# Score levels of a decayed scan: two heads in one product, with the odd heads' tokens held in reverse order

## The chip, the cores and the metric

The kernel runs on one core of a Trainium2 chip. The metric is the device time of one execution in microseconds; lower is better. The engines of the core work side by side and meet at semaphores: TensorE (PE; its weight loads are PEld), VectorE (DVE), ScalarE (ACT), GpSimd (POOL) and SyncE (SP), which issues loads.

## The reference, cut to what matters

The whole program is two transformer-like blocks over 1024 tokens of width 1024. The second block holds an HGRN2 scan (8 heads of 128 key channels and 128 value channels), which the change rewrites:

```python
def hgrn2_chunkwise(q, fpre, v, lb):      # S_t = diag(f_t) S_{t-1} + (1 - f_t) v_t^T,  o_t = S_t^T q_t
    q = silu(q)
    f = lb + (1 - lb) * sigmoid(fpre)     # per channel
    k = 1 - f
    logf = log(f)
    # per chunk, b = cumsum(logf):
    #   A[t, s] = sum_d q[t, d] * exp(b[t, d] - b[s, d]) * k[s, d]      for s <= t
    #   o       = (q * exp(b)) @ S + A @ v
    #   S       = exp(b_last) * S + (k * exp(b_last - b))^T @ v
```

The difference b[t] - b[s] is taken per channel, so A isn't one plain product of q and k. The reference uses chunks of 64 tokens; the kernel uses tiles of 128.

## The kernel before

The program is a list of stages; each engine has its own instruction list, and the classes below write them through their methods pe, act and dve. Weights are streamed: SP loads a strip of 256 columns, GpSimd splits it into a high and a low part (a cast, L2671, and a subtraction, L2673, for each half of the strip), and TensorE makes every projection of three products (L217 and L401). A strip's first product on TensorE frees the buffer of the strip before, and GpSimd then starts to split the next one.

**Feeding stage (HgInputs).** It makes, transposed (channels on partitions, 512 tokens along the free axis, one job for each head and half of the tokens), q = silu (ScalarE, L1894), k = 1 - f (VectorE, L1943) and b = a running sum of log f that restarts at each tile of 128 (VectorE's scan, L1945). Each goes to the scratch tensor hT_s in HBM (L1863). The constants of the later stages (LATE) are loaded here, from ScalarE's queue (L1874).

**The scan (Hgrn).** Eight tiles of 128 tokens, all eight heads side by side in tiles of 128 x 1024. A is built from seven levels: at level l the tokens are cut into blocks of 2 x 2^l, and only pairs (query in the upper half of a block, key in the lower) are taken. With mid = b at the last token of the lower half, the two factors exp(mid - b) on the keys and exp(b - mid) on the queries are both at most one. VectorE subtracts (L2170 elo for keys, L2171 eup for queries), ScalarE takes Exp over the whole buffer E (L2051), VectorE multiplies with k and q (L2177 klo, L2178 kup) into KQ, TensorE multiplies KQ of every head by itself (L2116, a0 to a6: eight f32 products of 128 x 128 x 128, each in two records in the trace), and VectorE copies the wanted places from PSUM into A under a mask (`pick`, L2212; A is cleared once a tile, L2160). a7 is k by q unchanged, for the diagonal. E, KQ and the PSUM pair are double-buffered by the level's parity, so VectorE runs subtract(l), multiply(l-1), pick(l-2) in turn.

Then, once a tile: qe = q exp(b) (L2185), kdif (L2186), an Exp (L2072), kd (L2188), eight transposes of kd (L2122, kdT), their copy back to SBUF (L2075, kdr), the output products (L2131 and L2132, o), the state products (L2137, ds), the head norm (L2080 on ScalarE, small steps, L2199 `on`), the state update (L2204), the store of `on` to m_s (L2089), and the loads of q, k, b of two tiles ahead (L2040, three DMAs) and of v (L2043). The stores and loads all stand in ScalarE's list.

**What fills TensorE meanwhile (Units).** 208 units, each one tile of 128 tokens by 256 columns of the remaining projections (24 products, L217), are laid out by hand between the scan's products: marks(t) says how many units are made before each of a0..a7, the transposes, o and the next tile. From tile 1 on there is one unit between two levels, three between a7 and the transposes, one between these and o, five behind o. Each unit goes to one of two PSUM banks and ScalarE copies it out (L1985); TensorE can be at most two units ahead of that copy (`self.kept`). ScalarE's list has the copies at fixed places between its other work. The retention stage and the closing stage follow and take up the rest of the units.

## Time and profile before

| what | value |
|---|---|
| median of 3 runs | 3329.5 us (3325.21 to 3337.8) |
| the profiled execution's own time | 3327.03 us |
| its span | 3325.2 us |
| TensorE busy | 2998.3 us, 90% |
| VectorE busy | 1707.6 us, 51% |
| ScalarE busy | 689.0 us, 21% |
| GpSimd busy | 1099.5 us, 33% |
| granted TensorE clock, mean | 0.949 |

Busy time is the time in which an engine has an instruction under way, and it overlaps between engines; TensorE's products are pipelined, so it is not a measure of how hard the array works. In lists in order of time, the first number is the start in us from the span's start, the second the duration; what stands in square brackets is the engine's idle time before it and who ended it.

### The profile page before, as it was taken

How to read it: one execution, taken by the hardware profiler on the slowest of the kernel's cores; microseconds unless marked ns; L12 is line 12 of the kernel's file. 1: busy time of each engine (PE TensorE's matmuls, PEld its weight loads, DVE VectorE, ACT ScalarE, POOL GpSimd, SP SyncE). 2: the span in 40 equal slices, each digit the busy share in tenths (PEclk: the TensorE clock that was granted, in tenths of full speed). 3: DMA queues.
4: the chain of work that ended last, by engine and by line, in shares of the span. 5: the costliest groups of instructions: out<-in, count | busy, mean ns of one | idle time of the engine just before them, and what ended most of it. 6: DMA issues, size and time to landing. Idle time of an engine off the chain costs nothing.

```text
span 3325.2 us, 43694 instructions
## 1 busy us (share of the span) xinstructions
PE 2998.3 (90%) x18988; PEld 2703.1 (81%) x18988; DVE 1707.6 (51%) x2127; ACT 689.0 (21%) x1178; POOL 1099.5 (33%) x588
## 2 busy tenths in 40 slices
PE   6999777787899999999999897998999999989987
PEld 6888767776887887777777776778999999978887
DVE  3589356765331265444444448713166656455445
ACT  3010011221332231000000003311122222234331
POOL 7342131102553353232223323653223232311343
PEclk9998798988899999999999998999999999999998
DMA  5122221101431242111111114443333233345662
GB/s 194 56 91 87 77 70 51 39 29 35 160 114 51 83 145 90 38 39 50 38 38 51 51 38 146 152 158 114 96 115 109 83 106 105 127 147 182 228 241 89
DMA packets 148072, 325.71 MB, mean 98 GB/s; under 512 B 11148, under 2 KB 77608, under 8 KB 147752
## 3 DMA queue, kind: packets, MB, share of 16 engines
q10 hardware_dynamic: 105832, 169.80, 15.0%
q1 hardware_dynamic: 42048, 153.11, 14.7%
q8 instruction: 150, 2.46, 0.3%
q14 instruction: 42, 0.34, 0.0%
HBM read 245.26 MB, written 77.61 MB: 97 GB/s over the span
## 4 chain that ended last, share of the span: by engine, by line
PE 72%; DVE 13%; issue 5%; ACT 4%; POOL 2%; ACTq 2%; DMA 1%; DVEq 0%
PE pp L217 23%; PE pp L202 20%; PE pp L401 7%; PE pp L1609 6%; PE pp L2116 3%; POOL w_lo L2673 2%; PE pp L1151 1%; PE pp L1160 1%; PE pp L1162 1%; PE pp L1519 1%; DVE gdn_C L1343 1%; PE pp L1499 1%; DVE ffn_cb L557 1%; POOL w_hi L2671 1%; DVE gdn_U L1322 1%
## 5 line engine op out<-in xcount | busy, mean ns | idle before, releaser
L2671 POOL CAST w_hi<-w_raw 128x1024 fp32r<-128x1024 f32 x292 | 349.0, 1195 | 2176.7 <-PE pp L217 957.8
L217 PE MATMUL pp<-w_hi,act_hi 128*128 128x256 f32 (+1 forms) x2752 | 801.3, 291 | 51.6 <-ACT hg_st L1985 22.6
L217 PE MATMUL pp<-w_lo,act_hi 128*128 128x256 f32 (+1 forms) x2752 | 788.9, 287 | 0.0
L217 PE MATMUL pp<-w_hi,act_lo 128*128 128x256 f32 (+1 forms) x2752 | 788.8, 287 | 0.0
L2673 POOL TENSOR_TENSOR w_lo<-w_raw,w_hi 128x1024 fp32r<-128x1024 f32 x292 | 758.4, 2597 | 23.4
L217 PEld LDWEIGHTS pp<-w_hi,act_hi 128*128 128x128 f32 x2752 | 542.9, 197 | 59.3 <-issue 24.2
L217 PEld LDWEIGHTS pp<-w_lo,act_hi 128*128 128x128 f32 x2752 | 542.7, 197 | 0.0
L217 PEld LDWEIGHTS pp<-w_hi,act_lo 128*128 128x128 f32 x2752 | 541.9, 197 | 0.0
L202 PE MATMUL pp<-act_hi,w_hi 128*128 128x512 f32 x960 | 295.7, 389 | 1.6 <-POOL w_lo L2673 1.6
L202 PE MATMUL pp<-act_lo,w_hi 128*128 128x512 f32 x960 | 295.6, 389 | 0.0
L202 PE MATMUL pp<-act_hi,w_lo 128*128 128x512 f32 x960 | 295.5, 389 | 0.0
L401 PE MATMUL pp<-act_hi,w_hi 128*128 128x512 f32 x448 | 182.3, 407 | 33.8 <-ACT hgin_f L1859 16.8
L202 PEld LDWEIGHTS pp<-act_hi,w_hi 128*128 128x128 f32 x960 | 180.1, 188 | 39.2 <-issue 1.8
L202 PEld LDWEIGHTS pp<-act_lo,w_hi 128*128 128x128 f32 x960 | 180.2, 188 | 37.5
L202 PEld LDWEIGHTS pp<-act_hi,w_lo 128*128 128x128 f32 x960 | 180.2, 188 | 37.5
L2212 DVE COPY_PREDICATED hg_A<-up_masks,pp 128x1024 f32<-128x1024 int32 x64 | 87.1, 1362 | 190.4 <-issue 190.4
L401 PE MATMUL pp<-act_lo,w_hi 128*128 128x512 f32 x448 | 179.7, 401 | 0.0
L401 PE MATMUL pp<-act_hi,w_lo 128*128 128x512 f32 x448 | 179.6, 401 | 0.0
L1609 PE MATMUL pp<-w_hi,ffn_gh 128*128 128x512 f32 x352 | 119.8, 423 | 48.3 <-DVE ffn_y L1777 38.2
L862 DVE SCALAR_TENSOR_TENSOR mixin_conv<-pp,mixin_cw,mixin_conv 128x1023 f32<-128x1023 f32 (+14 forms) x120 | 152.0, 1267 | 3.7
L1777 DVE TENSOR_TENSOR ffn_y<-ffn_y,pp 128x1024 f32<-128x1024 f32 x72 | 87.1, 1218 | 106.9 <-PE pp L1609 106.9
L1985 ACT ACTIVATE hg_st<-pp 128x256 f32<-128x256 f32 x208 | 77.5, 378 | 265.4 <-PE pp L217 231.1
(382 smaller groups left out, 4469.9 us busy)
## 6 DMA issues: line engine op xcount, KB each, us to landing
w_raw<-in_weights SPq DMA_DIRECT2D x292, 512.0 KB, 3.7
z_s<-hg_st ACTq DMA_DIRECT2D x24, 1024.0 KB, 4.6
hg_qkb<-hT_s ACTq DMA_DIRECT2D x24, 512.0 KB, 6.2
qkvT_s<-mixin_o ACTq DMA_DIRECT2D x12, 512.0 KB, 2.8
gdn_qkv<-qkvT_s ACTq DMA_DIRECT2D x8, 768.0 KB, 5.1
front_x<-in_x ACTq DMA_DIRECT2D x8, 512.0 KB, 6.7
mix_x<-in_x ACTq DMA_DIRECT2D x8, 512.0 KB, 5.7
x_s<-mix_y ACTq DMA_DIRECT2D x8, 512.0 KB, 2.9
```

Of the source, the lines that this page charges most:

```text
L202: last = pe.matmul(dst[:, h * hn:(h + 1) * hn], w[slot][:, k * SC + mt * P:k * SC + mt * P + P], a[:, k, h * hn:(h + 1) * hn], start=(k == ...
L217: last = pe.matmul(dst, a[:, k, t * P:(t + 1) * P], w[slot][:, k * SC:k * SC + n], start=(k == 0 and a is high and w is w_hi), stop=(k == ...
L401: last = pe.matmul(dst, w[slot][:, k * SC + mt * P:k * SC + mt * P + P], a[:, k, h * 512:(h + 1) * 512], start=(k == 0 and w is w_hi and a ...
L557: ins = dve.scalar_tensor_tensor(dst[:, j:T], src[:, 0:T - j], w(k), dst[:, j:T], ALU.mult, ALU.add)
L862: ins = dve.scalar_tensor_tensor(dst[:, j:T], pp[3][:, 0:T - j], w, dst[:, j:T], ALU.mult, ALU.add)
L1609: last = pe.matmul(dst[:, h * 512:(h + 1) * 512], a[gset][:, kk, t * P:(t + 1) * P], w[slot][:, kk * D + h * 512:kk * D + h * 512 + 512], ...
L1777: self.sums.done(dve.tensor_tensor(y, y, new, ALU.add), "sum")
L1985: act.activation(self.st[i % 2][:, t, :], self.dst(k), ACT.Copy).then_inc(self.kept, 1)
L2116: last = pe.matmul(pp[l % 2][:, h * P:(h + 1) * P], lhs[:, h, :], rhs[:, h, :], start=True, stop=True)
L2212: self.dves.done(dve.copy_predicated(self.A[:, :, :], up_masks[:, l, :].rearrange("p (a n) -> p a n", a=1).broadcast_to((P, HH, P)), pp[l ...
L2671: pool.tensor_copy(hi, raw).then_inc(w_split, 1)
L2673: pool.tensor_tensor(lo, raw, hi.bitcast(F32), ALU.subtract).then_inc(w_ready, 1)
```

## The change

Only one half of the places of a level's product of a head with itself is used: queries are in upper halves, keys in lower ones. If another head's tokens are held in reverse order, its upper and lower halves change places, so one product can serve two heads: the stationary operand holds head j's keys in its lower places and the odd head's queries in the others, the moving operand the reverse. The change does this:

- The weights' columns of v, and the rows of hT_s, are ordered even heads first, odd heads behind (on the host, and by the store's address). Odd heads' q, k and b are written backwards within 512 tokens (`kept`), so a tile of an odd head is read from the mirrored place; the three loads of a tile become six of half the size.
- A level's operations on E and KQ are of the same sizes as before but take their operands from both halves with access patterns of one more dimension. At level 0 the keys' factor is one, so their subtraction is left out, the multiply is a copy, and Exp runs over half of E.
- a0 to a6 are four products; the picks copy 128 x 512 into a buffer `both` under masks that are symmetric. A is no longer cleared. a7 is unchanged.
- `join`: the diagonal of a7 into A by two multiplications with the identity, then two predicated copies out of `both`, upper places for even heads and lower ones, written backwards, for odd heads.
- qe is made in two operations, the odd heads' written backwards (so the queries of o are in true order).
- v of the odd heads is turned round by a product with a reversed identity (`turn_back`, jv) and copied back by ScalarE (vr); one of the five units behind o now stands between jv and o.
- The store of `on` becomes two stores which put the heads back into order.
- Small buffers move, one more constant is loaded in LATE, `both` is cleared once.

```diff
@@ LATE @@
-        LATE = [(up_masks, "c_up"), (ret_decay, "c_decay"), (ret_xi, "c_xi"), (ret_zeta, "c_zeta"), (ret_gc, "c_gc"),
+        LATE = [(up_masks, "c_up"), (turn_back, "c_back"), (ret_decay, "c_decay"), (ret_xi, "c_xi"), (ret_zeta, "c_zeta"), (ret_gc, "c_gc"),
...
+            def kept(self, x, j):
+                return backwards(x[:, :]) if j % 2 else x[:, :]
...
-                    self.qs.done(act.activation(self.q[j % 4][:, :], bank(2 * (j % 4)), ACT.Silu), "q")
+                    self.qs.done(act.activation(self.kept(self.q[j % 4], j), bank(2 * (j % 4)), ACT.Silu), "q")
...
-                    V.done(dve.tensor_scalar(self.k[s][:, :], f, -1.0, 1.0, ALU.mult, ALU.add), "k")
+                    V.done(dve.tensor_scalar(self.kept(self.k[s], j), f, -1.0, 1.0, ALU.mult, ALU.add), "k")
...
-                    V.done(dve.tensor_tensor_scan(self.b[s][:, :], self.keep[:, :], self.l[s][:, :], 0.0, ALU.mult, ALU.add), "b")
+                    V.done(dve.tensor_tensor_scan(self.kept(self.b[s], j), self.keep[:, :], self.l[s][:, :], 0.0, ALU.mult, ALU.add), "b")
@@ Hgrn.act @@
-                        act.dma_start(self.qkb[s][:, j, :, :], hT_s[j].rearrange("(h p) n -> p h n", p=P)[:, :, t * P:(t + 1) * P]).then_inc(self.loaded[s], 16)
+                        for odd in range(2):
+                            at = t if odd == 0 else t // 4 * 4 + 3 - t % 4
+                            heads = slice(odd * HH // 2, (odd + 1) * HH // 2)
+                            act.dma_start(self.qkb[s][:, j, heads, :], hT_s[j].rearrange("(h p) n -> p h n", p=P)[:, heads, at * P:(at + 1) * P]).then_inc(self.loaded[s], 16)
...
-                    after(act, V, f"eup{l}", t)
-                    A.done(act.activation(self.E[l % 2][:, :, :], self.E[l % 2][:, :, :], ACT.Exp), f"x{l}")
+                    after(act, V, f"er{l}", t)
+                    e = self.E[l % 2][:, :, :] if l else self.E[0][:, HH // 2:HH, :]
+                    A.done(act.activation(e, e, ACT.Exp), f"x{l}")
...
                     U.keep_to(act, m[9])
+                    after(act, PE, "jv", t)
+                    A.done(act.activation(self.v[t % 2][:, HH // 2:HH, :], bank(1).rearrange("p (h e) -> p h e", h=HH // 2), ACT.Copy), *(("xk", "kdr", "vr") if last else ("vr",)))
+                    U.keep_to(act, m[9] + 1)
                     after(act, PE, "o", t)
...
-                    act.dma_start(m_s[t * P:(t + 1) * P, :], self.on[:, :, :].rearrange("p h e -> p (h e)")).then_inc(self.stored, 16)
+                    for odd in range(2):
+                        act.dma_start(m_s[t * P:(t + 1) * P, :].rearrange("p (h two e) -> p h two e", two=2, e=P)[:, :, odd, :],
+                                      self.on[:, odd * HH // 2:(odd + 1) * HH // 2, :]).then_inc(self.stored, 16)
@@ Hgrn.pe @@
-                        for h in range(HH):
-                            last = pe.matmul(pp[l % 2][:, h * P:(h + 1) * P], lhs[:, h, :], rhs[:, h, :], start=True, stop=True)
+                        dst, keys = pp[l % 2], self.KQ[l % 2]
+                        if l < LEVELS:
+                            for j in range(HH // 2):
+                                last = pe.matmul(dst[:, j * P:(j + 1) * P], keys[:, j, :], keys[:, HH // 2 + j, :], start=True, stop=True)
+                        else:
+                            for h in range(HH):
+                                last = pe.matmul(dst[:, h * P:(h + 1) * P], self.qkb[s][:, 1, h, :], self.qkb[s][:, 0, h, :], start=True, stop=True)
...
+                    last = pe.matmul(bank(1), turn_back[:, :], self.v[s][:, HH // 2:HH, :].rearrange("p h e -> p (h e)"), start=True, stop=True)
+                    PE.done(last, *(("jv",) if t + 1 < NT else ("kdT", "jv")))
+                    U.make_to(pe, m[9] + 1)
+                    after(pe, A, "vr", t)
@@ Hgrn.dve @@
-                    V.done(dve.memset(self.A[:, :, :], 0.0), "zero")
...
-                            mid = bv[:, :, 0, sz - 1:sz].broadcast_to((P, nb, sz))
-                            V.done(tt(ev[:, :, 0, :], mid, bv[:, :, 0, :], ALU.subtract), f"elo{l}")
-                            V.done(tt(ev[:, :, 1, :], bv[:, :, 1, :], mid, ALU.subtract), f"eup{l}")
+                            mid = at_steps(b, sz - 1, rows(sz), [HALF_ + 1, 2], [0, sz])
+                            if l:
+                                V.done(tt(as_keys(e, sz), mid, of_keys(b, sz), ALU.subtract), f"el{l}")
+                            V.done(tt(as_queries(e, sz), of_queries(b, sz), mid, ALU.subtract), f"er{l}")
...
+                            if l:
+                                V.done(tt(as_keys(kq, sz), of_keys(k, sz), as_keys(e, sz), ALU.mult), f"klo{l}")
+                            else:
+                                V.done(dve.tensor_copy(as_keys(kq, sz), of_keys(k, sz)), "klo0")
+                            V.done(tt(as_queries(kq, sz), of_queries(q, sz), as_queries(e, sz), ALU.mult), f"kup{l}")
...
-                    self.pick(dve, t, LEVELS)
+                    self.join(dve, t)
...
+            def join(self, dve, t):
+                V, n = self.dves, HH // 2
+                raw = pp[LEVELS % 2][:, :].rearrange("p (h n) -> p h n", h=HH)
+                unit = ident[:, :].rearrange("p (a n) -> p a n", a=1).broadcast_to((P, n, P))
+                after(dve, self.pes, f"a{LEVELS}", t)
+                V.done(dve.tensor_tensor(self.A[:, 0:n, :], raw[:, 0:n, :], unit, ALU.mult), "dg0")
+                V.done(dve.tensor_tensor(backwards(self.A[:, n:HH, :]), raw[:, n:HH, :], unit, ALU.mult), "dg1")
+                after(dve, V, "dg1", t)
+                V.done(dve.memset(self.mark[:, :], 0.0), "ata")
+                V.done(dve.copy_predicated(self.A[:, 0:n, :], self.mask(LEVELS), self.both[:, :, :]), "cpa")
+                V.done(dve.copy_predicated(backwards(self.A[:, n:HH, :]), self.mask(LEVELS + 1), self.both[:, :, :]), "cpb")
```

## Rows read from the trace of the kernel before

**Rows 1.** The page, busy time and share of the span.
```profile
PE 2998.3 (90%) x18988; PEld 2703.1 (81%) x18988; DVE 1707.6 (51%) x2127; ACT 689.0 (21%) x1178; POOL 1099.5 (33%) x588
```
**Rows 2.** By stretches: us, PE, PEld, DVE, ACT, POOL busy, clock, DMA share, GB/s.
```profile
2487.53:2554.75 67.22, 66.79 (x569) 66.58 (x569) 42.39 (x64) 17.04 (x30) 18.23 (x8) 1.00 0.35 103
2554.75:2622.02 67.27, 66.78 (x568) 66.58 (x568) 42.37 (x63) 17.03 (x30) 18.23 (x8) 1.00 0.34 103
```
**Rows 3.** The chain that ended last, in time: start us, us, engine, line, records.
```profile
1101.09 3.46 PE pp L1499 x16
...
2507.53 1.78 PE pp L2116 x16
2509.31 2.88 PE pp L217 x24
```
**Rows 4.** Waits of TensorE, 2255 to 2890: total us, times, longest us.
```profile
PE pp L217 <- ACT hg_st L1985: 2.3, 6, 0.7
PE pp L2122 <- DVE hg_KQ L2188: 1.3, 1, 1.3
```
**Rows 5.** VectorE in one level, in time, and L2170 by itself (min/median/max ns).
```profile
2513.44 0.67 DVE L2178 TENSOR_TENSOR hg_KQ<-hg_qkb,hg_E 128x512 f32<-128x512 f32 x1
2514.05 1.34 DVE L2212 COPY_PREDICATED hg_A<-up_masks,pp 128x1024 f32<-128x1024 int32 x1
...
2515.30 0.67 DVE L2177 TENSOR_TENSOR hg_KQ<-hg_qkb,hg_E 128x512 f32<-128x512 f32 x1
...
L2170 DVE TENSOR_TENSOR hg_E<-hg_qkb x56: 628/678/2869, 2263.6 to 2845.7; 128x512 f32<-128x512 f32 x56
```
**Rows 6.** In time: VectorE beside GpSimd, within the levels of tile 2.
```profile
2502.95 2.70 POOL L2673 TENSOR_TENSOR w_lo<-w_raw,w_hi 128x1024 fp32r<-128x1024 f32 x1
2503.34 2.86 DVE L2177 TENSOR_TENSOR hg_KQ<-hg_qkb,hg_E 128x512 f32<-128x512 f32 x1
2506.12 0.68 DVE L2178 TENSOR_TENSOR hg_KQ<-hg_qkb,hg_E 128x512 f32<-128x512 f32 x1
```
**Rows 7.** In time: between a7 and the output products, tile 2.
```profile
2529.24 1.21 DVE L2185 TENSOR_TENSOR hg_KQ<-hg_qkb,hg_E 128x1024 f32<-128x1024 f32 x1
2530.37 1.21 DVE L2186 TENSOR_TENSOR hg_E<-hg_qkb 128x1024 f32<-128x1024 f32 x1
2532.57 2.40 POOL L2673 TENSOR_TENSOR w_lo<-w_raw,w_hi 128x1024 fp32r<-128x1024 f32 x1
2532.71 3.34 DVE L2188 TENSOR_TENSOR hg_KQ<-hg_qkb,hg_E 128x1024 f32<-128x1024 f32 x1 [1.13 <-ACT hg_E L2072]
2536.42 1.04 PE L2122 MATMUL pp<-ident,hg_KQ 128*128 128x128 f32 x8
2537.49 1.03 ACT L2075 ACTIVATE hg_E<-pp 128x1024 f32<-128x1024 f32 x1 [3.31 <-PE pp L2122]
```
**Rows 8.** Tile end: in time; L2040's three issues (min/median/max ns); then the chain.
```profile
2482.34 3.03 ACTq L2040 DMA_DIRECT2D hg_qkb<-hT_s  x3
2484.32 0.91 DVE L2160 MEMSET hg_A<- 128x1024 f32 x1 [0.38 <-DVE hg_S L2204]
2485.40 1.65 ACTq L2043 DMA_DIRECT2D hg_v<-z_s  x1
2489.07 0.69 DVE L2178 TENSOR_TENSOR hg_KQ<-hg_qkb,hg_E 128x512 f32<-128x512 f32 x1
...
L2040 ACTq DMA_DIRECT2D hg_qkb<-hT_s x3: 392/1062/1520, 2482.3 to 2483.9; - x3
...
2487.53 6.01 PE pp L217 x48
2493.55 1.78 PE pp L2116 x16
```
**Rows 9.** Feeding stage: L1943 by itself (min/median/max ns); one issue from the chain.
```profile
L1943 DVE TENSOR_SCALAR hgin_k<-hgin_f x16: 426/428/2505, 2080.3 to 2176.3; 128x512 f32<-128x512 f32 x16
...
2072.42 0.45 ACTq L1874
```

More of the change, by code:

```diff
@@ L147, in build @@
         late_end = top["at"]
+        spare = {"at": spare_at}
+        turn_back, both = place("turn_back", [P, P], F32, spare), place("both", [P, HH // 2, P], F32, spare)
         w_raw = place("w_raw", [P, STRIP])
@@ L187, in full, with backwards, at_steps @@
             return t[tuple(slice(None) for _ in t.shape)]
+        def backwards(x):
+            (step, n), off = x.ap[-1], x.offset
+            return bass.AP(x.tensor, off + step * (n - 1), [*[list(a) for a in x.ap[:-1]], [-step, n]])
+        def at_steps(x, first, *steps):
+            return bass.AP(x.tensor, x.offset + first, [list(x.ap[0]), *[list(a) for a in steps]])
         def weights_ready(pe, j):
@@ L2021, in __init__ @@
                 self.sm = b("sm", [P, 6, HH])
+                self.both = both
                 self.loaded = [sem(f"hg_loaded{s}") for s in range(2)]
@@ L2139, in pe @@
                     else:
-                        PE.done(last, "kdT", "o")
+                        PE.done(last, "o")
                     U.make_to(pe, m[10])
@@ L2723, in shape_constants @@
         low[:, l] = m
-        up[:, l] = m.T
-    up[:, LEVELS] = np.eye(P)
+        up[:, l] = m | m.T
+    up[:, LEVELS], up[:, LEVELS + 1] = np.triu(np.ones((P, P)), 1), np.tril(np.ones((P, P)), -1)
     h = np.arange(HH)
```

93 lines of the change are left out of this document (53 added, 40 removed).

## The prediction

> **What bounds the kernel now.** I read the page first: TensorE is busy for 90% of the span [rows 1]. Shares are an average over stages, so the second view is the table by stretches over the stage that is changed (2255 to 2892 us), cut at the same point of successive token tiles [rows 2]. A tile takes 67.22 us there, and TensorE is busy in 66.79 of them at granted clock 1.00, the upper of its two levels (2.4 GHz); VectorE in 42.39. So TensorE's instructions are the bound, and every one removed counts if nothing else comes due. The chain shows what they are [rows 3]: per level 1.78 us of score products (eight heads, 16 records) and 2.88 us of a projection unit (24 records), 4.66 us together. The list of waits [rows 4] has TensorE idle here, beside the first load, for 2.3 us behind ScalarE's evictions, at tile ends, and 1.3 us once before the transposes of L2122. Three covers are thin, and the change touches all of them.
>
> **Products halved (56 levels).** Each of the seven levels of eight tiles issues four products in place of eight; the diagonal one (a7) keeps eight. What is a product's cost? In attention 16 f32 records of 256 columns take 3.46 us [rows 3], 0.216 each, 0.108 for 128 columns; 16 of those are 1.73, against 1.78 seen, so 0.05 to 0.08 us belongs to the change from one kind of product to the other and stays. Eight records less are 8 x 0.108 = 0.87 us a level, 56 x 0.87 = **48.4 us saved** (49.8 if the 1.78 simply halves). A level then takes 2.88 + 0.92 = 3.80 us.
>
> **The turning product (jv), added.** One product of 512 moving columns in f32, two records, once a tile. The trace has none so wide; by the 256-column row a record is 0.43 us, so 0.86 plus 0.08 for the switch, **7.5 us for eight tiles**. From below it can't be under two fp32r records of 512 columns at the 2.88/24 = 0.12 us per 256 of the units [rows 3]: 0.5 us, 4 us in all. I take 7.5. ScalarE copies its result back (vr: half of the 1.03 us of L2075 [rows 7], about 0.6), under the unit of 2.88 us that the diff puts between jv and o; it is covered unless ScalarE is late there by over 2 us. TensorE's own balance is 48.4 - 7.5 = **40.9 us**.
>
> **VectorE in the levels.** Starts of its operations are 0.60 us apart for 512 elements and 1.25 for the predicated copy of 1024 [rows 5], so a level costs 4 x 0.60 + 1.25 = 3.65 us of 4.66. After: four operations of the same size (the access patterns gain a dimension), and a predicated copy of 512. Operations of two SBUF inputs are 1.13 us apart for 1024 elements (qe to kdif [rows 7]) and 0.60 for 512, so 512 elements are worth 0.53 and the copy 1.25 - 0.53 = 0.72 us. Sum 3.1 us of 3.80. Cover stays, 0.7 a level where it was 1.0. Level 0 loses its key half (no el0, a copy for klo0, half an Exp), and the clearing of A (0.91 [rows 8]) goes: these shorten the tile's head by some 2 us.
>
> What eats into cover is GpSimd [rows 6]: while its subtraction of 2503.0 to 2505.7 runs, VectorE's 0.6 us product ends only 2.86 us after its start. That happens once in every tile's levels, since TensorE's strip boundary starts it. I replayed VectorE's order with these: the key/query product for level 3 ended 0.7 us before TensorE needed it (2506.8 against 2507.5 [rows 3, 6]); with the faster cadence it ends about 0.3 us late. **2 us for the tiles 1 to 7**; ends 0 (another operation is caught) and 7 (a microsecond each). The Trainium skill, "SBUF — State Buffer", under "Who interferes with whom", says that a VectorE instruction with two SBUF inputs contends with a GpSimd one that reads SBUF, the later one blocking fully. By that rule, the trace agrees [rows 6]; it would also let the two new copies that merge `both` into A, whose inputs lie in SBUF, be caught, which would take the join below to its upper end and no further.
>
> **The join, before the transposes.** Behind a7 VectorE does today: pick 1.25, qe 1.13, kdif 1.2, wait for an Exp, kd 3.34 (blocked as above), ending at 2536.05 [rows 7]; TensorE, which has three units (8.64 us) in between, begins the transposes at 2536.42. Slack 0.3 us. The change puts two products (0.6 each) and two predicated copies (0.7) in place of the pick: 2.7 for 1.25, and splits qe (no cost but 0.07): +1.5 us. But kd waits for GpSimd until about 2535 anyway (2532.57 + 2.40 [rows 7]); GpSimd's subtraction itself would start later by about 0.7 us, behind kdif. So the delay of kd is between 0 and 1.5; I take 0.8, 0.5 after the slack, for tiles 1 to 6: 3 us; tile 0 has no slack (the 1.3 us of [rows 4]) and pays 1.5: **4.5 us**, ends 0 and 9.
>
> **The tile's end, on ScalarE's queue.** The chain runs through it [rows 8]: three loads 3.03 us, load of v 1.65, then the eviction for which TensorE has waited. o moves one unit later, and so does this eviction, so TensorE has the same 8.65 us of cover, with one unit instead of two behind it before a0: 2.9 us less for er0, x0 and kup0. Today kup0 ends 3.8 us before a0 (2489.76 against 2493.55 [rows 8]); with the 2 us gained at the head it still ends about a microsecond early. The queue: one store becomes two, in pieces of 512 B, three loads become six of half the size. The first load issues in 0.39 us, the later ones in 1.06 and 1.52: they wait for the traffic in front, 512 KB in some 1.5 us, not for their own issuing. If that is all, six halves take what three take. If each is a wait of its own the block grows by 0.1 for the store and up to 1.5. I take 0.6 for six tiles: **3.6 us**, ends 0 and 9.6. The Trainium skill, "DMA: Bandwidth & Descriptors", section "Why small descriptors are slow (HBM only)", gives each packet a fixed overhead, which speaks against a store cut into 512 B pieces; no store of before is cut so, and the sum leaves it out.
>
> **The feeding stage (2075 to 2255) and the start.** Odd heads are written backwards by Silu, by the scan and by `1 - f`. The last takes 0.43 us for 512 elements [rows 9], where the level's operations of 512 take 0.68 [rows 5]; backwards it may fall to that: eight times 0.25, half of it on the chain. The late constants gain one issue of 0.45 us, on the chain too. **1.5 us**, ends 0 and 4. Loads of the first tile are cut in six: **0.5 us**, ends 0 and 3. The Trainium skill, "Vector Engine (DVE) Microarchitecture Reference", in section 5.1 "Performance modes — why throughput varies by op and dtype", lists operands with a negative step as not measured, and no row of before has one. Zeroing `both` once runs under the first load. The table of weights is reordered on the host and costs nothing; later stages see the same tiles, shifted.
>
> **The sum.** 40.9 - 2 - 4.5 - 3.6 - 1.5 - 0.5 = 28.8 us. The profiled execution took 3327.0 us (span 3325.2), 2.5 below the median of 3329.5. 3327.0 - 28.8 = 3298.2, and with a part of that offset I say **3299 us**.
>
> **Rivals.**
> (a) *All covers hold*: kd is bound by GpSimd, the queue by traffic. Then nearly the whole 40.9 arrives: 3287 us. For it: both mechanisms are in the rows. Against: slacks of 0.3 us. Chance 0.18.
> (b) *The hand-offs take most of it*: ends of the ranges for join (9), queue (9.6), levels (7) and the feeding stage (4) together leave 40.9 - 29.6 = 11 us: 3316 us, within 0.5%. For it: each of them waits at a point where TensorE already idles. Chance 0.13.
> (c) *VectorE becomes the bound, and the kernel is slower.* The place is the seven levels; the mechanism is that reads alternating between two far places, with rows of 1, 2 or 4 elements, or with a mid repeated per row, don't keep the pace of 0.60 us for 512 elements. The level is 3.80 us of TensorE, so it decides from (3.80 - 0.76)/4 = 0.76 us an operation, and the kernel is slower than before from 0.97. At half rate (1.13) a level costs 4 x 1.13 + 0.76 = 5.3 against 4.66: 49 levels of tiles 1 to 7 lose 31 us, jv and the join add some 15, tile 0, whose levels are 16 us long, still gains 6: 3367 us. Against it: today's level 0 works on single elements two apart, level 1 on pairs, and the operation's times over all levels are 0.63 at the least and 0.68 in the median [rows 5]. Chance 0.07.
> (d) *It doesn't do what it says*: the cost is per level and not per record, so fewer products save nothing. Then 3340. Against: 1.78 for 16 records [rows 3] and 1.04, tail included, for the 8 records of the transposes [rows 7]. Chance 0.02.
>
> **Chances and range.** The forecast itself, 3290 to 3310, has 0.60, (a) 0.18, (b) 0.13, (c) and (d) 0.09. Half a per cent, 16.6 us, is about what a measurement here tells from no change. The forecast and (a) lie beyond it on the fast side, a little of (b) too: faster 0.80, same 0.12, slower 0.08. The range takes in (a) with 3 us for the runs' scatter and (b): 3284 to 3318.
>
> **What would show it.** Score products of a level in 0.9 us, tiles 1 to 6 62.0 (all covers hold: 67.2 - 7 x 0.87 + 0.94) to 63.5 us apart instead of 67.2; TensorE's count down by 56 x 8 records and up by 16. The join: TensorE waiting before the transposes with kd as the releaser. The queue: waits at the unit behind o, ended by ScalarE's eviction, over 0.5 us. The levels: waits of L2116's products on the query product near the third level. Rival (c) shows as operations of the levels above 0.76 us and TensorE idle in every level. The prediction is wrong in its core if the tiles are still 66 us apart, or if clock falls below 1.00 in them because of the new waits.

## The result: slower, 3357.7 us where 3299 was forecast

| | before | after |
|---|---|---|
| median of five runs each | 3329.5 us (3321.2 to 3337.8) | 3357.65 us (3354.6 to 3358.5) |
| span of the profiled execution | 3325.2 us | 3356.2 us |
| granted TensorE clock, mean | 0.949 | 0.941 |
| the changed stage, from the issue of its first load to the next stage's first transposes | 2254.7 to 2892.4 | 2251.6 to 2920.9 |

The ratio is 1.0084, with a 95% interval of 1.0063 to 1.0104. So the change costs 28 us, and by the stage's ends all of it is lost in the scan (+31.6 us; the stages ahead of it are 3 us shorter, those behind it 2.5 longer).

The page of the changed kernel, its first block: TensorE has 432 records fewer (56 levels x 8 fewer, 16 more), as the diff says, and is busy 22.8 us less than in [rows 1], in a span 31 us longer. VectorE is busy 20.7 us more, although it has less to do: an operation that is held up counts as busy.

```profile
PE 2975.5 (89%) x18556; PEld 2673.0 (80%) x18556; DVE 1728.3 (51%) x2144; ACT 689.6 (21%) x1186; POOL 1074.2 (32%) x588
```

**The products did get cheaper.** From the chain of the changed kernel, in time (start, duration), inside the levels of tile 1, and the turning product:

```profile
2440.45 0.89 PE pp L2139 x8
2441.34 2.88 PE pp L227 x24
...
2476.14 0.86 PE pp L2152 x2
```

A level's products take 0.89 us for 8 records where [rows 3] had 1.78 for 16. jv (L2152) takes 0.86. That is 56 x 0.89 = 49.8 us saved and 8 x 0.86 = 6.9 spent: 42.9 us to the good on TensorE.

**But TensorE waits.** The waits of TensorE over the stage, 2250 to 2920 (total us, times, longest), to be held against 2.3 and 1.3 us in [rows 4]:

```profile
PE pp L227 <- ACT hg_st L1999: 30.6, 12, 3.7
PE pp L2139 <- DVE hg_mark L2269: 15.3, 7, 2.2
PE pp L227 <- DMA hg_qkb<-hT_s: 11.2, 1, 11.2
PE pp L2148 <- DVE hg_KQ L2241: 6.9, 1, 6.9
```

Without the first load these are 52.8 us against 3.6. By the times of the single waits they fall at three places of every tile: ahead of a projection unit behind a7 (3.7 us, six times) and once ahead of the transposes (6.9, tile 0); ahead of a level's products (2.2, seven times); and at the tile's end (0.7 to 1.7, six times, 8.3 us in all). (L227 is a projection unit, L2139 a level's products, L2148 the transposes; a wait put down to `hg_mark` is one for VectorE's work ahead of it.)

**The join, in time.** VectorE, GpSimd and ScalarE of the changed kernel behind a7 of tile 1 (start, duration; the same place in a tile as [rows 7]):

```profile
2460.52 1.54 DVE L2234 TENSOR_TENSOR hg_KQ<-hg_qkb,hg_E 128x512 f32<-128x512 f32 x1
2461.98 3.39 DVE L2239 TENSOR_TENSOR hg_E<-hg_qkb 128x1024 f32<-128x1024 f32 x1
2466.49 3.30 DVE L2241 TENSOR_TENSOR hg_KQ<-hg_qkb,hg_E 128x1024 f32<-128x1024 f32 x1 [1.12 <-ACT hg_E L2091]
```
```profile
2460.37 1.15 POOL L2740 CAST w_hi<-w_raw 128x1024 fp32r<-128x1024 f32 x1 [26.08 <-PE pp L227]
2461.59 2.69 POOL L2742 TENSOR_TENSOR w_lo<-w_raw,w_hi 128x1024 fp32r<-128x1024 f32 x1
...
2466.34 2.36 POOL L2742 TENSOR_TENSOR w_lo<-w_raw,w_hi 128x1024 fp32r<-128x1024 f32 x1
```
```profile
2465.40 1.06 ACT L2091 ACTIVATE hg_E<-hg_E 128x1024 f32<-128x1024 f32 x1 [9.46 <-DVE hg_E L2239]
2466.36 0.36 ACT L1999 ACTIVATE hg_st<-pp 128x256 f32<-128x256 f32 x1
```

In the kernel before, at the same place of tile 2, the cast began when kdif (2530.37 in [rows 7]) was already under way:

```profile
2531.01 1.48 POOL L2671 CAST w_hi<-w_raw 128x1024 fp32r<-128x1024 f32 x1 [25.36 <-PE pp L217]
```

Read the starts. GpSimd's cast begins 0.15 us ahead of the second half of qe (L2234), which takes 1.54 instead of 0.68 us. Its subtraction begins 0.39 us ahead of the difference kdif (L2239), which takes 3.39 where [rows 7] has 1.21. The exponential xk (L2091) can begin only at 2465.40, and behind it in ScalarE's list stands the eviction of a projection unit (L1999). TensorE may be two units ahead of the evictions and no more: it stands still from 2463.05 to 2466.78. kd (L2241) is caught as it was before.

Tile 0 is another case. There GpSimd starts earlier against VectorE, and what is caught are the two copies out of `both` and the first half of qe (2.96, 1.55 and 2.82 us, where tile 1 has 0.76, 0.73 and 0.69). kd is late by this, and TensorE waits the 6.9 us ahead of the transposes:

```profile
2386.58 2.96 DVE L2282 COPY_PREDICATED hg_A<-up_masks,both 128x512 f32<-128x512 int32 x1
```

**And its clock falls.** The table by stretches around that idle time (us, busy time of PE, PEld, DVE, ACT, POOL, granted clock, DMA share, GB/s), and the unit that follows, from the chain:

```profile
2460.00:2463.00 3.00, 3.00 (x26) 2.85 (x24) 3.00 (x4) 0.00 (x0) 2.55 (x2) 1.00 0.00 0
2463.00:2466.00 3.00, 0.06 (x1) 0.00 (x0) 2.37 (x1) 0.60 (x1) 3.00 (x2) 0.93 0.23 48
2466.00:2469.00 3.00, 2.22 (x10) 2.22 (x11) 2.51 (x1) 1.11 (x3) 2.62 (x2) 0.50 0.80 279
2469.00:2472.00 3.00, 3.00 (x16) 3.00 (x15) 0.78 (x1) 0.00 (x0) 0.00 (x0) 0.50 1.05 285
```
```profile
2466.78 5.49 PE pp L227 x24
```

The granted clock goes from 1.00 to 0.50, the lower of its two levels (1.2 GHz), and the unit takes 5.49 us instead of 2.88. So the place costs 3.73 + 2.61 = 6.3 us a tile, 38 us over tiles 1 to 6.

**The levels.** The same meeting, inside the levels of tile 1 (VectorE, then GpSimd, in time):

```profile
2426.91 0.93 DVE L2214 TENSOR_TENSOR hg_E<-hg_qkb 128x512 f32<-128x512 f32 x1
2427.76 2.87 DVE L2215 TENSOR_TENSOR hg_E<-hg_qkb 128x512 f32<-128x512 f32 x1
2430.55 1.52 DVE L2222 TENSOR_TENSOR hg_KQ<-hg_qkb,hg_E 128x512 f32<-128x512 f32 x1
2431.99 2.84 DVE L2225 TENSOR_TENSOR hg_KQ<-hg_qkb,hg_E 128x512 f32<-128x512 f32 x1
```
```profile
2427.37 2.71 POOL L2742 TENSOR_TENSOR w_lo<-w_raw,w_hi 128x1024 fp32r<-128x1024 f32 x1
...
2431.61 2.68 POOL L2742 TENSOR_TENSOR w_lo<-w_raw,w_hi 128x1024 fp32r<-128x1024 f32 x1
```

Both halves of a strip are split here, and both subtractions catch a VectorE operation. Together with the two slowed by casts it is 5.4 us over the pace of 0.60, and the level's products come 2.2 us late. In the kernel before only one was caught [rows 6], because the first meeting went the other way round: there GpSimd's first subtraction in the levels was the one held up, in each of tiles 1 to 7 (4.73 to 4.75 us), and VectorE's operations beside it kept their 0.67 to 0.70. In tile 2:

```profile
2496.64 4.74 POOL L2673 TENSOR_TENSOR w_lo<-w_raw,w_hi 128x1024 fp32r<-128x1024 f32 x1
```

VectorE's L2170 has the same start, 2496.64, and in the other tiles the two starts lie within 0.02 us of each other. In the changed kernel the first subtraction took 2.71 us and VectorE paid.

The clock falls behind some of the levels' waits, not behind all. The products and the unit behind the wait in tile 1 and in tile 2, from the chain:

```profile
2434.89 2.07 PE pp L2139 x8
2436.96 3.49 PE pp L227 x24
...
2508.32 1.16 PE pp L2139 x8
2509.47 2.88 PE pp L227 x24
```

Tiles 1, 5 and 7 are of the first kind (1.5 us each), tiles 2, 3, 4 and 6 of the second, with the clock at 1.00, all behind waits of 2.18 or 2.19 us.

The account then closes. The products give 42.9 us; the waits take 49.2 more than before; the slow units at the join take 6 x 2.61 = 15.7. That is 22.0 of the stage's 31.6 us. The clock falls at five more places: behind the three waits in the levels (4.6 us in all), once at a tile's end (2711.3 to 2714.7, 1.5 us) and at tile 0's join (1.97 + 3.32 us for the transposes and the unit, where the kernel before has 1.09 + 2.88: 1.3 us). And a level's products take 1.16 us behind a wait even at 1.00, in place of 0.89: 1.9 us over seven. Together this is 31.3 of the 31.6.

### The profile page after: what moved, and what is told of

It reads as the page before. It is cut to its first block, busy times and chain, and to the rows that moved or that the text cites. A ratio compares the mean times of both kernels' runs of the same rounds, so it can differ in the third digit from the quotient of the medians.

```text
span 3356.2 us, 42873 instructions
## 1 busy us (share of the span) xinstructions
PE 2975.5 (89%) x18556; PEld 2673.0 (80%) x18556; DVE 1728.3 (51%) x2144; ACT 689.6 (21%) x1186; POOL 1074.2 (32%) x588
## 4 chain that ended last, share of the span: by engine, by line
PE 70%; DVE 17%; ACT 4%; issue 2%; POOL 2%; ACTq 2%; DMA 2%; DVEq 0%
PE pp L227 23%; PE pp L212 19%; PE pp L411 7%; PE pp L1619 6%; POOL w_lo L2742 2%; PE pp L2139 1%; PE pp L1161 1%; PE pp L1170 1%; PE pp L1172 1%; PE pp L1529 1%; DVE hg_KQ L2225 1%; DVE hg_E L2215 1%; PE pp L1509 1%; DVE gdn_C L1353 1%; ACTq L2058 1%
## 5 line engine op out<-in xcount | busy, mean ns | idle before, releaser
L2740 POOL CAST w_hi<-w_raw 128x1024 fp32r<-128x1024 f32 x292 | 340.5, 1166 | 2232.9 <-PE pp L227 1013.8
L227 PE MATMUL pp<-w_hi,act_hi 128*128 128x256 f32 (+1 forms) x2752 | 813.6, 296 | 82.1 <-ACT hg_st L1999 52.7
L227 PE MATMUL pp<-w_lo,act_hi 128*128 128x256 f32 (+1 forms) x2752 | 796.7, 289 | 0.0
L227 PE MATMUL pp<-w_hi,act_lo 128*128 128x256 f32 (+1 forms) x2752 | 796.4, 289 | 0.0
L2742 POOL TENSOR_TENSOR w_lo<-w_raw,w_hi 128x1024 fp32r<-128x1024 f32 x292 | 741.4, 2539 | 23.4
L227 PEld LDWEIGHTS pp<-w_hi,act_hi 128*128 128x128 f32 x2752 | 551.1, 200 | 92.6 <-ACT hg_st L1999 53.6
L227 PEld LDWEIGHTS pp<-w_lo,act_hi 128*128 128x128 f32 x2752 | 551.0, 200 | 2.0 <-issue 1.9
L227 PEld LDWEIGHTS pp<-w_hi,act_lo 128*128 128x128 f32 x2752 | 550.0, 200 | 0.0
L212 PEld LDWEIGHTS pp<-act_hi,w_hi 128*128 128x128 f32 x960 | 180.1, 188 | 39.2 <-issue 1.7
L411 PEld LDWEIGHTS pp<-act_hi,w_hi 128*128 128x128 f32 x448 | 87.9, 196 | 55.8 <-issue 27.9
L1999 ACT ACTIVATE hg_st<-pp 128x256 f32<-128x256 f32 x208 | 77.4, 377 | 266.8 <-PE pp L227 227.7
```

The lines of the kernel that those rows point to most:

```text
L212: last = pe.matmul(dst[:, h * hn:(h + 1) * hn], w[slot][:, k * SC + mt * P:k * SC + mt * P + P], a[:, k, h * hn:(h + 1) * hn], start=(k == ...
L227: last = pe.matmul(dst, a[:, k, t * P:(t + 1) * P], w[slot][:, k * SC:k * SC + n], start=(k == 0 and a is high and w is w_hi), stop=(k == ...
L411: last = pe.matmul(dst, w[slot][:, k * SC + mt * P:k * SC + mt * P + P], a[:, k, h * 512:(h + 1) * 512], start=(k == 0 and w is w_hi and a ...
L1999: act.activation(self.st[i % 2][:, t, :], self.dst(k), ACT.Copy).then_inc(self.kept, 1)
L2740: pool.tensor_copy(hi, raw).then_inc(w_split, 1)
L2742: pool.tensor_tensor(lo, raw, hi.bitcast(F32), ALU.subtract).then_inc(w_ready, 1)
```

## Experiments

Times are medians, ratios are to the kernel before on the same chip; the interval is 95%. The kernel before took 3326.1 us beside the first four, 3328.0 beside the next four, 3325.1 beside the last four. In the traced executions the scan begins anywhere from 2247.8 to 2262.9 us, in an order that doesn't follow the edits, so where medians don't settle a small difference, the length of the changed stage in the trace is given too: 637.7 us in the kernel before, 669.3 in the changed one. It is one execution each.

### Two more copies in the kernel before

```diff
                     self.pick(dve, t, LEVELS)
+                    for i in range(2):
+                        after(dve, V, f"cx{i - 1}" if i else f"cp{LEVELS}", t)
+                        hs = slice(i * HH // 2, (i + 1) * HH // 2)
+                        V.done(dve.copy_predicated(self.A[:, hs, :], up_masks[:, LEVELS, :].rearrange("p (a n) -> p a n", a=1).broadcast_to((P, HH // 2, P)),
+                                                   pp[LEVELS % 2][:, :].rearrange("p (h n) -> p h n", h=HH)[:, hs, :]), f"cx{i}")
```

> The kernel before, with two more predicated copies of half the size (about 0.72 us each, so 1.45 us) put between the last pick of a tile and the product of q with the decays; nothing else is changed. This is the extra VectorE work that the changed kernel has at this place, alone. Theory (the join is a cliff): the moved product meets GpSimd's cast and the difference meets GpSimd's subtraction, the exponential xk comes late, ScalarE's eviction queued behind it comes late, TensorE stands still and its clock falls: 3.5 to 6 us a tile over 7 tiles, so 25 to 40 us slower than before, 3355 to 3370 us. Rival (the added time counts as it is, on a path that was already the bound): 1.45 us times 8 tiles, at most 12 us slower, about 3340 us. Second rival (it is hidden by the units): no change, 3330 us.

3350.6 us, ratio 1.0065 (1.0050 to 1.0079): 24.5 us slower, twice the 8 x 1.5 = 12 us of VectorE's work that was added. The rival's bound is passed and the theory's 25 to 40 just missed. Of its mechanism the wait is there in every tile, the clock's fall only in some. VectorE and TensorE of this kernel, tile 2, in time, and the stretch behind; then the unit behind the wait in tiles 2 and 3, from the chain:

```profile
2535.75 2.08 DVE L2191 TENSOR_TENSOR hg_E<-hg_qkb 128x1024 f32<-128x1024 f32 x1
...
2539.25 0.39 PE L217 MATMUL pp<-w_hi,act_hi 128*128 128x256 f32 x1 [1.72 <-ACT hg_st L1985]
```
```profile
2540.00:2543.00 3.00, 3.00 (x17) 3.00 (x17) 1.14 (x1) 0.08 (x1) 2.92 (x3) 0.56 0.97 314
```
```profile
2539.25 4.62 PE pp L217 x24
...
2609.93 3.14 PE pp L217 x24
```

The difference is slowed by the cast to 2.08 us, and TensorE is idle for 1.72 us ahead of a unit in each of tiles 1 to 6. In tiles 2 and 5 the clock falls behind that (0.56 in the stretch shown) and the unit takes 4.62 us; in the other four it stays at 1.00 and the unit takes 3.14. So two tiles lose 3.5 us and four lose 2.0. Tile 0 loses 5.4: TensorE waits 4.4 us for kd where it was 1.3, and the transposes and the unit behind them, at the lower clock, take 6.3 us where they took 4.0. Together this is 20 us, and the stage is 20.2 longer (657.9). The traced execution was the fastest of the six (3345.5 us), so no trace shows where the rest of the median's 24.5 lies. Nothing of the change is in this kernel but the length of its join, and a loss at the join is there, with 2.0 or 3.5 us a tile where the changed kernel has 6.3. The meeting itself is a lighter one (the cast, not the subtraction, catches the difference).

### The eviction ahead of the wait

```diff
+                        U.keep_to(act, m[8] - 1)
                         after(act, V, "kdif", t)
                         A.done(act.activation(self.E[0][:, :, :], self.E[0][:, :, :], ACT.Exp), "xk")
-                        U.keep_to(act, m[8] - 1)
```

> The changed kernel, with ScalarE's eviction of the projection unit ahead of the transposes placed before its wait for the difference kdif instead of behind the exponential xk. TensorE can then make the next unit before it reaches the transposes. Theory: the idle of 3.7 us at 2463.05 and the fall of the clock behind it go from this place; part comes back as a wait for kd ahead of the transposes, since the join itself stays as long as it is. Net 10 to 20 us faster than the changed kernel: 3338 to 3348 us. Rival (the wait only moves to the transposes in full, clock fall too): 3355 to 3360 us.

3368.9 us, ratio 1.0109 (1.0092 to 1.0127): above both expectations, with an interval that overlaps the changed kernel's. The stage itself is only 2.2 us longer than there (671.5); of the 11.7 us between the two traced executions 7.7 lie ahead of the scan, which this edit doesn't touch. So nothing was won, as the rival said, and whether the edit costs anything isn't shown. The first row of TensorE's waits in this kernel, and its chain:

```profile
PE pp L2148 <- DVE hg_KQ L2241: 30.4, 7, 6.9
```
```profile
2473.62 3.29 DVE hg_KQ L2241
2476.95 1.97 PE pp L2148 x8
2478.93 4.56 PE pp L227 x24
```

The wait moved whole to the transposes, and the clock fell there, in tile 1 with 1.97 us of transposes in it too. In the changed kernel the late eviction does a service: TensorE's stop ahead of the unit lets that unit stand, as cover, behind xk and beside kd. So the wait follows the length of a7-to-kd on VectorE, and ScalarE's order only says where it shows.

### The merge ahead of a7

```diff
                 after(dve, V, f"cp{LEVELS - 1}", t)
+                V.done(dve.tensor_tensor(self.A[:, 0:n, :], self.both[:, :, :], sides[:, 0:1, :].broadcast_to((P, n, P)), ALU.mult), "dg0")
+                V.done(dve.tensor_tensor(backwards(self.A[:, n:HH, :]), self.both[:, :, :], sides[:, 1:2, :].broadcast_to((P, n, P)), ALU.mult), "dg1")
                 after(dve, self.pes, f"a{LEVELS}", t)
...
-                V.done(dve.copy_predicated(self.A[:, 0:n, :], self.mask(LEVELS), self.both[:, :, :]), "cpa")
-                V.done(dve.copy_predicated(backwards(self.A[:, n:HH, :]), self.mask(LEVELS + 1), self.both[:, :, :]), "cpb")
+                V.done(dve.copy_predicated(self.A[:, 0:n, :], self.mask(LEVELS), raw[:, 0:n, :]), "cpa")
+                V.done(dve.copy_predicated(backwards(self.A[:, n:HH, :]), self.mask(LEVELS), raw[:, n:HH, :]), "cpb")
```

Its `up_masks[:, LEVELS]` is the unit matrix, `sides` holds the two triangles as numbers.

> The changed kernel, with the two halves of the score block merged ahead of a7: before TensorE's unmasked product, VectorE multiplies the picked levels with a float mask of each direction into the two halves of A; behind a7 it only copies the two diagonals under one mask. The number of VectorE instructions is the same (two of 0.6 us move ahead of a7, two predicated copies of 0.7 stay behind it). Theory: 1.2 to 1.4 us less stands between a7 and the products with the decays; if that lets them miss GpSimd's cast and subtraction, the exponential xk is in time, and about 6 us a tile over 6 tiles comes back: 3315 to 3330 us. Rival (only the moved time counts): 8 us faster, 3350 us. If the products still meet GpSimd: 3350 to 3360 us.

3322.8 us, ratio 0.9984 (0.9971 to 0.9996): 1.0% of the time below the changed kernel, for 1.3 us a tile moved (10 us): inside the theory's 3315 to 3330, far from the rival's 3350. The stage takes 634.3 us. The difference now begins ahead of GpSimd's cast, in tile 1 (VectorE, then GpSimd, in time):

```profile
2456.49 1.22 DVE L2241 TENSOR_TENSOR hg_E<-hg_qkb 128x1024 f32<-128x1024 f32 x1
2458.84 3.34 DVE L2243 TENSOR_TENSOR hg_KQ<-hg_qkb,hg_E 128x1024 f32<-128x1024 f32 x1 [1.13 <-ACT hg_E L2093]
```
```profile
2457.07 1.54 POOL L2743 CAST w_hi<-w_raw 128x1024 fp32r<-128x1024 f32 x1 [26.04 <-PE pp L229]
```

kd is still caught, as in the kernel before, and TensorE waits there 4.4 us in tile 0 only. The level waits (15.3 us, seven) are untouched.

### Subtractions of the next level placed ahead of the pick

```diff
+                    subtract(0)
+                    subtract(1)
                     for st in range(1, LEVELS + 2):
...
...
+                        subtract(st + 1)
                         l = st - 2
                         if l >= 0:
                             self.pick(dve, t, l)
```

> The changed kernel, with the two subtractions of the next level placed ahead of the pick and of the products of the level before, so that ScalarE's exponential starts earlier. Theory: the level loop's seven waits of TensorE (15.3 us together in the stage) and the dip of the clock behind them go: 12 to 20 us faster than the changed kernel, 3338 to 3346 us. Rival (the waits in the levels are covered by the longer join, and what is won there is waited for at the join): 0 to 5 us, 3353 to 3358 us.

3358.7 us, ratio 1.0082 (1.0065 to 1.0099): nothing won by the median. (The traced execution is the shortest of six, 3347.1 us against 3356.1 to 3363.1, and its stage is 10 us shorter than the changed kernel's, 659.1: the join of tile 3 doesn't stall in it, and the clock falls behind two waits in the levels, not three.) TensorE waits 13.4 us in seven in the levels, where it was 15.3; both subtractions of GpSimd still catch one of VectorE's operations each. This other order within VectorE's levels doesn't avoid the meetings. The rival's number was right, its reason not: the waits weren't covered elsewhere, they stayed.

### The turning product ahead of the transposes

```diff
                     U.make_to(pe, m[8])
+                    pe.wait_ge(self.v_loaded[s], 16 * (t // 2 + 1))
+                    after(pe, V, f"cp{LEVELS - 1}", t)
+                    last = pe.matmul(bank(1), turn_back[:, :], self.v[s][:, HH // 2:HH, :].rearrange("p h e -> p (h e)"), start=True, stop=True)
+                    PE.done(last, "jv")
                     after(pe, V, "kd" if t + 1 < NT else "qe", t)
```

> The changed kernel, with the product jv that turns the odd heads' values placed ahead of the transposes and its copy out (vr) ahead of the copy of the turned keys, so that the projection unit between them is not needed any more and five units again stand behind o, as before the change. Theory (the join's VectorE work is the cause, not where jv stands): no more than 5 us either way, 3352 to 3362 us, with ScalarE's list slightly later at the transposes. Rival (the displaced unit and the split of the tail cost a good part of the change's loss): 15 us or more faster, 3342 us or less.

3360.9 us, ratio 1.0095 (1.0079 to 1.0110): no difference from the changed kernel that can be told, and the stage is as long (669.1). Where jv stands, and the unit taken from behind o, are no cause.

### The loads out of the tile's end

```diff
                         level(t, l)
+                        if t and t + 1 < NT and 2 <= l < 5:
+                            load(t + 1, (4 - l,))
+                        if t and t + 1 < NT and l == 5:
+                            load_v(t + 1)
...
-                        if t + 2 < NT:
-                            load(t + 2)
-                            load_v(t + 2)
```

> The changed kernel, with the six loads and the load of v taken out of ScalarE's tail of a tile and issued two at a time behind the exponentials of levels 2 to 5 of the next tile; the waits and sizes are the same. Theory (the issue of the loads, 4.5 us at 2416.90 to 2421.59, stands on the path into the next tile's levels, and TensorE waits for the eviction behind it 1.2 us a tile): 6 us times 1.2 to 2, so 7 to 15 us faster than the changed kernel, 3342 to 3350 us. Rival (the levels' start is covered by the units behind o, and the first level only comes earlier for nothing): 0 to 3 us faster, 3354 to 3358 us.

3349.8 us, ratio 1.0068 (1.0051 to 1.0085): 0.16% below the changed kernel, with intervals that overlap. By the medians it is 7.8 us, inside the theory's 7 to 15, and the stage is 7.6 us shorter (661.7). TensorE's waits on the eviction fall from twelve to six, the ones at the join:

```profile
PE pp L227 <- ACT hg_st L1999: 22.4, 6, 3.7
```

8.2 us less, which is what stood at the tile's end.

### GpSimd's split held until kd is done

The cast and the subtraction of the strip that falls into the join do the same work, later; this takes the meeting away and leaves the join as long as the change made it. The same hold was put into the kernel before.

```diff
                 if j:
                     pool.wait_ge(w_used, j)
+                if j in held:
+                    after(pool, hg.dves, "kd", held[j])
```

> The changed kernel, with GpSimd's cast and subtraction of the weight strip that falls into the join held back until VectorE has finished kd of that tile; the work is the same, only later. Theory (the loss at the join is contention between VectorE and GpSimd, with the eviction and TensorE's clock behind it): the products take 0.6 us, the difference 1.2 and kd 1.2 again, the exponential comes about 4 us earlier, the 3.7 us wait and the fall of the clock go, 6 us a tile over 6 to 7 tiles: 3315 to 3325 us. Rival (the join is too long by its own four instructions, contention or none): 3345 us or more.

> The kernel before, with the same hold: GpSimd's cast and subtraction of the strip that falls into the join wait for kd. Theory: the join before the change met only kd with the subtraction (3.34 against 1.2 us) and TensorE waited little for it, so little is won, 0 to 6 us: 3323 to 3329 us. Rival (contention at the join costs the kernel before as much as the changed one, and is no cause of the difference): 20 us or more faster, 3309 us or less.

The changed kernel: 3321.8 us, ratio 0.9978 (0.9968 to 0.9987), 1.06% below what it was. The kernel before: 3326.8, ratio 0.9992 (0.9980 to 1.0003), nothing. The theory holds on both, and the rival falls: with all four instructions of the join in place, the loss at the join is gone but for 0.7 us a tile. In the chain of the changed kernel with the hold, tile 1:

```profile
2460.12 1.14 DVE hg_E L2239
...
2462.67 3.14 PE pp L227 x24
```

That 0.71 us is the idle time ahead of the unit, and the clock stays at 1.00 behind it. The stage takes 631.7 us, 37.6 less, which is the 38 us of the six joins. The seven waits of 2.2 us in the levels are all still there, and here the clock falls behind five of them.

### Both splits held

The strip that begins with a tile is held too, until the last level's products (kup6) are made; TensorE needs it eight units later.

```diff
+                    if at == hg.units.strips[i][2] and (n >= hg.marks(t)[7] or t and n < hg.marks(t)[1]):
+                        held[hg.units.strips[i][0] + 1] = ("kd" if n >= hg.marks(t)[7] else f"kup{LEVELS - 1}", t)
```

> The changed kernel with the hold at the join as before, and GpSimd's split of the strip that begins with a tile held too, until VectorE has made the last level's products (kup6). VectorE then meets GpSimd neither in the levels nor at the join. Theory (the seven waits of 2.2 us in the levels are the same contention): they go, 15 us off the kernel with the hold at the join alone (3322), so 3300 to 3312 us. Rival (GpSimd's later split makes the weights late for the strip at the join, or VectorE's levels are too long by themselves): 3318 us or more.

> The kernel before with both holds. Theory: before the change TensorE waited for nothing in the levels and 1.3 us in all at the join, so nothing is won: 3322 to 3330 us, and the changed kernel with both holds stands 15 to 28 us below it. Rival (the contention costs both kernels the same): 3310 us or less.

The changed kernel: **3297.7 us**, ratio 0.9910 (0.9896 to 0.9924). The kernel before: 3326.1, ratio 0.9998 (0.9988 to 1.0007). TensorE's waits over the stage in the changed kernel with both holds, and GpSimd, with its idle time and who ended it:

```profile
PE pp L227 <- ACT hg_st L1999: 13.8, 13, 1.8
...
PE pp L2139 <- DVE hg_mark L2269: 2.2, 1, 2.2
PE pp L2148 <- DVE hg_KQ L2241: 1.7, 1, 1.7
```
```profile
2433.44 1.04 POOL L2748 CAST w_hi<-w_raw 128x1024 fp32r<-128x1024 f32 x1 [37.63 <-DVE hg_KQ L2225]
...
2451.07 1.04 POOL L2748 CAST w_hi<-w_raw 128x1024 fp32r<-128x1024 f32 x1 [10.67 <-DVE hg_KQ L2241]
```

Six of the seven waits in the levels are gone; the one left is in the last tile, which was given no hold. The change, put into a kernel in which GpSimd keeps out of VectorE's way, brings 3326.1 - 3297.7 = 28.4 us (26.5 by the lengths of the stage, 636.3 and 609.8). Put into the kernel as it was, it costs 28.2.

### With the loads later, and with the merge early

These have both holds and the edit of the loads; the second has the early merge as well.

> The changed kernel with both holds and with the loads of qkb and v issued behind the exponentials of levels 2 to 5. Theory: the gains add, 7 to 10 us below the kernel with both holds: 3292 to 3303 us. Rival (with the waits in the levels gone the tail is covered): no change against both holds.

3288.8 us, ratio 0.9896 (0.9878 to 0.9914).

> The changed kernel with both holds, the loads behind the levels, and the halves merged ahead of a7. Theory: with GpSimd out of the way the join costs at most 0.7 us a tile of TensorE's time, so the merge brings 0 to 5 us more: 3288 to 3300 us, below both kernels. Rival (the merge keeps its 34 us without contention too): 3270 us or less.

3283.6 us, ratio 0.9876 (0.9858 to 0.9894): 1.2% below the kernel before and 2.1% below the changed one, the fastest here. The intervals of these two overlap with each other, and the first's with that of both holds alone, so their own shares, 9 and 5 us, aren't settled by times. The traces agree with them. The stage takes 609.8 us with both holds, 600.3 with the loads later and 593.5 with the merge too. The waits on evictions, 2250 to 2880, are 13.8, 5.8 and 1.6 us; the 1.6 is one wait that ends at 2876.67, in the next stage. Two a7 of the last kernel in its chain:

```profile
2514.81 1.78 PE pp L2145 x16
...
2575.93 1.78 PE pp L2145 x16
```

A tile takes 61.1 us, against 67.2 in [rows 2] and 70.9 to 75.1 in the changed kernel. That the merge is worth 34 us in one kernel and 5 in the other (7 by the stage) shows how little the worth of an edit is its own.

## Why the prediction was wrong

- **Products halved: right.** 0.89 us a level against 0.92 forecast, 49.8 us saved against 48.4. **jv: right**, 6.9 us against 7.5. vr takes 0.60 us and is covered.
- **VectorE's pace: right**, and rival (c) with its slow access patterns falls. The forecast of 0.60 us between starts held for every new pattern. Minimum, median and maximum in ns of the level's subtraction, of the diagonal written backwards, and of `1 - f` in the feeding stage:

```profile
L2215 DVE TENSOR_TENSOR hg_E<-hg_qkb x56: 673/686/2883, 2259.9 to 2876.0; 128x512 f32<-128x512 f32 x56
...
L2279 DVE TENSOR_TENSOR hg_A<-pp,ident x8: 678/680/680, 2385.9 to 2891.3; 128x512 f32<-128x512 f32 x8
...
L1957 DVE TENSOR_SCALAR hgin_k<-hgin_f x16: 426/428/2516, 2077.3 to 2173.2; 128x512 f32<-128x512 f32 x16
```

  The feeding stage thus cost nothing, where 1.5 us was set down; the Trainium skill, "Vector Engine (DVE) Microarchitecture Reference", section 5.1, lists negative steps as not measured, and here they are at no cost for these three, as the rows show. That (c) named the right sign, slower, is an accident: its place was right in part, its mechanism was not.
- **The join: wrong, and the step that decided.** The prediction had kd "between 0 and 1.5" us late, because "GpSimd's subtraction itself would start later by about 0.7 us, behind kdif". This is what failed. GpSimd's start is set by TensorE (the strip's boundary lies between a7 and the transposes) and did not move with VectorE's work: its cast begins 4.85 us behind the start of a7 in both kernels, and its subtraction came 0.3 us earlier than before, not 0.7 later. VectorE, which began qe 1.3 us later behind a7 than before, now found cast and subtraction already under way. The one that starts second waits for the first: kdif, begun 0.39 us behind the subtraction, took 3.39 us. The rule of the Trainium skill quoted there ("SBUF — State Buffer", "Who interferes with whom") says just this, and the trace agrees. It was applied to kd, to the levels and to the two copies out of `both`, but not to qe and kdif, the two operations that the shift pushes over GpSimd's start. Of the two copies it said that this "would take the join below to its upper end and no further". They were caught in tile 0 alone. The upper end was 9 us for the stage, and the join's waits took 29 us and their clock 17 more.
- **Two things behind it were not in the sum at all.** First, the eviction queued behind xk on ScalarE: the prediction counted three units as TensorE's cover up to the transposes, while TensorE gets the third only after that eviction. Second, TensorE's clock. The prediction named its fall as what would make it "wrong in its core", and gave it no price. It came, at 2.6 us a tile behind the join.
- **The levels: the right mechanism, the wrong size.** 2 us, at most 7, was forecast; 15.3 us came as waits, in tiles 1 to 7, and 4.6 us of clock behind three of them. The replay had one operation caught in each tile's levels, as in [rows 6]. In the changed kernel VectorE is at a different point when GpSimd starts, loses the first meeting too, and is caught by both subtractions. What moved it there (the shorter copy, or the tile's head) isn't separated by a run.
- **The tile's end: undersized.** 3.6 us was forecast, 0 to 9.6 its bounds; 8.3 us of waits came. The six issues take 3.7 us where three took 3.03 [rows 8], each 0.53 to 0.71 us, the two stores 1.2 where one took 0.34: each issue cost its own half microsecond. The load of v behind them is shorter in part, and at the end of tile 0 the whole block takes 6.0 us where it took 5.0.
- **Its sum stands where the contention doesn't.** 28.8 us was forecast, 28.4 was measured between the two kernels with both holds, with tiles 62.2 to 63.9 us apart (62.0 to 63.5 forecast). Part of that is luck, since the levels, the join and the queue's terms don't match one by one there either: the join still waits 0.7 us a tile, the tile's end 1.3.

The 56.6 us between -28.4 and +28.2 are therefore what VectorE's and GpSimd's meetings cost the changed kernel and not the one before. The clock's share in it is 23 us by the sum above (15.7 + 4.6 + 1.5 + 1.3), but no run separates it: no kernel here has the idle time of 3.7 us without the fall.

## What to carry to other kernels

An edit that shortens TensorE's work and moves VectorE's by a microsecond changes which of VectorE's operations meet GpSimd's. So list all of GpSimd's starts beside VectorE's new times and price each meeting, in both orders, at the whole length of the operation that came first; then follow who queues behind the one caught (here difference, exponential, eviction, unit), and price TensorE's clock wherever it would stand still in a stage that otherwise runs at 1.00. Where the meetings decide, it is cheaper to give GpSimd a wait that keeps it out (here two kinds of wait, 60 us) than to shorten VectorE's chain.

## What was not expected of the hardware

- The length of TensorE's idle time alone doesn't say whether the clock falls. In the changed kernel it was 0.50 behind all six idle times of 3.72 us at the joins (the unit took 5.49 us instead of 2.88) and behind three of the seven of 2.19 us in the levels; with the hold at the join it fell behind five of the seven of 2.19; with two more copies, behind two of six of 1.72 us (the unit took 4.62 us, and 3.14 in the other four); with both holds, behind none of the six of 0.71 us. Where it fell, it cost 1.5 us behind idle times of 1.7 to 2.2 us and 2.6 behind those of 3.72. What decides between equal idle times isn't settled here.
- GpSimd's own subtraction suffers or gains by the same meetings. It takes 2.38 us where it meets none of VectorE's operations (both holds, tile 1), 2.7 where it begins ahead of a VectorE operation and catches it, and 3.22 where it begins behind one (two more copies, tile 2, 2536.84). It can lose to more than one: in the kernel before, at 2496.64, it took 4.74 us, 2.36 more than alone, while VectorE ran four operations of two SBUF inputs at its pace of 0.60 (4 x 0.60 = 2.4).
- Issuing a load on ScalarE's queue took 0.53 to 0.71 us each for 256 KB, against 0.39, 1.06 and 1.52 us for three of 512 KB: six halves took longer than three wholes.
